# Token slices outermost in the dense units: the loop order of split_unit in a two-layer hybrid decoder step

## What is computed

```python
def ffn(x, norm_g, w_gu, w_down):
    h = rmsnorm(x, norm_g)
    g, u = jnp.split(h @ w_gu, 2, axis=-1)
    return x + (jax.nn.silu(g) * u) @ w_down
...
        x = x + jnp.concatenate([o_nsa, o_ssm], axis=-1) @ w_out    # layer 0
        q, kv = split_cols(h @ w_in, (SWA_WIDTH, SWA_KV_WIDTH))     # layer 1
        x = x + o.reshape(b, L, SWA_WIDTH) @ w_out                  # layer 1
```

## Time and profile before

| | |
|---|---|
| timed runs, median of 3 | 2853.9 us (2848.88 to 2857.44) |
| profiled execution, its own time | 2846.38 us |
| its span, first to last instruction | 2844.7 us |
| mean granted TensorE clock | 0.996 |
| TensorE matmul busy | 2795.5 us (98%) |
| TensorE weight load busy | 2543.5 us (89%) |
| VectorE busy | 1012.2 us (36%) |
| ScalarE busy | 645.6 us (23%) |
| GpSimd busy | 732.7 us (26%) |

### The profile page before, as it was taken

How to read it: one execution, slowest core, us unless ns; L and a number is a source line. 1 busy time by engine, 2 the same in 40 slices (tenths; PEclk the granted TensorE clock), 3 DMA queues, 4 the chain that set the end, 5 groups by cost and what they waited for, 6 DMA issues and landing times.

```text
span 2844.7 us, 44686 instructions
## 1 busy us (share of the span) xinstructions
PE 2795.5 (98%) x18772; PEld 2543.5 (89%) x18772; DVE 1012.2 (36%) x2137; ACT 645.6 (23%) x1344; POOL 732.7 (26%) x495
## 2 busy tenths in 40 slices
PE   8999999999999999999999999999999999999999
PEld 6866676667689999999999999879999999999998
DVE  3122356776553322222222251383432222222224
ACT  4021223666532100000000031284200000000004
POOL 1430000212322222222222231244222222222221
PEclk9999999999999999999999999999999999999999
DMA  7764112100631111111111112100111111111111
GB/s 236 196 178 148 51 31 67 46 29 1 197 108 45 45 45 45 45 45 45 45 45 45 45 45 51 39 17 16 45 45 45 45 45 45 45 45 45 45 60 64
DMA packets 205898, 179.73 MB, mean 63 GB/s; under 512 B 36730, under 2 KB 186287, under 8 KB 205106
## 3 DMA queue, kind: packets, MB, share of 16 engines
q1 hardware_dynamic: 195184, 144.20, 17.0%
q0 software_dynamic: 7616, 30.14, 3.5%
q10 hardware_dynamic: 2898, 2.54, 0.3%
HBM read 162.44 MB, written 19.51 MB: 64 GB/s over the span
## 4 chain that ended last, share of the span: by engine, by line
PE 71%; DVE 2%; ACT 1%; issue 0%; POOL 0%; DVEq 0%; POOLq 0%; ACTq 0%
PE ps L2262 55%; PE ps L2278 4%; PE ps L2298 4%; PE ps L2966 1%; PE ps L2686 1%; PE ps L2546 1%; PE ps L2667 1%; PE ps L2650 1%; PE ps L1911 1%; PE ps L1899 1%; PE ps L1946 0%; DVE arena L2775 0%; DVE arena L2373 0%; PE ps L1928 0%; PE ps L2957 0%
## 5 line engine op out<-in xcount | busy, mean ns | idle before, releaser
L2262 PE MATMUL ps<-spot,w_hi 128*128 128x368 f32 (+1 forms) x6156 | 1185.3, 327 | 1.5 <-DVE arena L2389 0.8
L2262 PEld LDWEIGHTS ps<-spot,w_hi 128*128 128x128 f32 x6156 | 1035.4, 188 | 2.3 <-DVE arena L2389 1.4
L2262 PE MATMUL ps<-spot,w_lo 128*128 128x368 f32 (+1 forms) x3132 | 686.0, 327 | 0.0
L2262 PEld LDWEIGHTS ps<-spot,w_lo 128*128 128x128 f32 x3132 | 537.3, 188 | 0.0
L2231 POOL CAST w_hi<-arena 128x2048 fp32r<-128x2048 f32 x78 | 151.8, 1946 | 1337.0 <-DMA arena<-in_w_gate_up 761.8
L2239 POOL TENSOR_TENSOR w_lo<-arena,w_hi 128x2048 fp32r<-128x2048 f32 x77 | 359.5, 4669 | 6.2
L2389 DVE TENSOR_TENSOR arena<-arena,ps 128x368 f32<-128x368 f32 (+1 forms) x312 | 147.0, 526 | 426.3 <-PE ps L2262 354.9
L601 PE MATMUL ps<-arena 128*128 128x368 f32 (+1 forms) x768 | 241.3, 472 | 0.0
L2487 ACT ACTIVATE arena<-arena 128x1088 f32<-128x1088 f32 x44 | 49.0, 1114 | 831.4 <-DVEq L2503 831.4
L601 PEld LDWEIGHTS ps<-arena 128*128 128x128 f32 x768 | 144.9, 191 | 86.0 <-issue 3.6
L2507 DVE TENSOR_TENSOR arena<-arena,ps 128x368 f32<-128x368 f32 x132 | 62.3, 527 | 443.5 <-PE ps L2262 438.3
(11 more groups left out here) (465 smaller groups left out, 3003.3 us busy)
## 6 DMA issues: line engine op xcount, KB each, us to landing
arena<-in_w_gate_up SPq DMA_DIRECT2D x88, 512.0 KB, 4.7
arena<-in_w_down SPq DMA_DIRECT2D x22, 1024.0 KB, 4.9
arena<-in_cache_nsa_slc_kv SPq DMA_DIRECT2D x112, 128.0 KB, 2.6
arena<-in_cache_nsa_cmp_kv SPq DMA_DIRECT2D x109, 128.0 KB, 2.3
arena<-in_w_in_even SPq DMA_DIRECT2D x9, 1024.0 KB, 7.1
x_spill<-arena POOLq DMA_DIRECT2D x1, 4352.0 KB, 14.2
arena<-in_x_prompt SPq DMA_DIRECT2D x8, 512.0 KB, 6.4
arena<-in_cmp_w_k POOLq DMA_DIRECT2D x16, 256.0 KB, 4.3
```

Of the source, the lines that this page charges most:

```text
L2262: mm = nc.tensor.matmul(ps[:, 3 * s + j, 0:b - a], w, x[:, a:b], start=m == 0, stop=m == len(order) - 1)
```

## The change

In `split_unit` the loop over the three slices becomes the outermost one. For each slice, all of k and hh, hl, lh run, and then the next slice follows. The optional hook `before` would be called in the first slice alone. `start` and `stop` of the accumulation keep their conditions, now once for each slice's own sequence. The other functions are the same.

```diff
@@ -2253,12 +2253,12 @@
 
             E.unit_start(s)
             order = [(kind, k) for k in range(n) for kind in ("hh", "hl", "lh")]
-            for m, (kind, k) in enumerate(order):
-                if before:
-                    before(kind, k)
-                (wh, wl), (xh, xl) = w_of(k), x_of(k)
-                w, x = {"hh": (wh, xh), "hl": (wh, xl), "lh": (wl, xh)}[kind]
-                for j, (a, b) in enumerate(SPLIT):
+            for j, (a, b) in enumerate(SPLIT):
+                for m, (kind, k) in enumerate(order):
+                    if before and j == 0:
+                        before(kind, k)
+                    (wh, wl), (xh, xl) = w_of(k), x_of(k)
+                    w, x = {"hh": (wh, xh), "hl": (wh, xl), "lh": (wl, xh)}[kind]
                     mm = nc.tensor.matmul(ps[:, 3 * s + j, 0:b - a], w, x[:, a:b], start=m == 0, stop=m == len(order) - 1)
             mm.then_inc(unit_ready[s], 1)
 
```

## The result

| | before | changed |
|---|---|---|
| timed runs, median | 2854.7 us (5 runs, 2848.9 to 2871.3) | 2840.8 us (5 runs, 2836.0 to 2842.7) |
| ratio of the runs | | 0.9944, 95% interval 0.9916 to 0.9972 |
| profiled execution, span | 2844.7 us | 2840.9 us |
| same pair timed again later | 2849.9 us (22 runs, 2841.4 to 2866.4) | 2843.6 us (12 runs, 2837.0 to 2848.6) |
| ratio, again | | 0.9986, 95% interval 0.9973 to 0.9998 |

Ratios and intervals are those on record; the quotients of the medians are 0.9951 and 0.9978. The change made the kernel a little faster, by 0.6% in the first comparison and by 0.1% in the second (the two intervals reach from 0.0 to 0.8%), where I had forecast 2859 us, no measurable difference, and a chance of 0.12 for faster. 2840.8 us lies just under the range (2842 to 2873).

What follows compares the result with a forecast made beforehand. TensorE's matmul spacing at L2262 was taken as the bound. Kept counts, waits and weight loads cost 0; the interpolated spacing adds 12.5 us to the profiled 2846.4 us, giving 2859 us, range 2842 to 2873.

Steps and rivals of the forecast that it cites:

- What bounds the kernel: TensorE, busy 98% of the span; an edit to L2262 in `split_unit` can change only the spacing of its matmuls.
- part 1: What is kept in `split_unit`: 9504 matmuls, as many loads, all waits and releases, the other engines' orders; cost nothing.
- the eviction cover: Three eviction additions, 1.43 us, stay hidden behind the next unit, at least 2.96 us; if lost, up to 1.43 us per unit.
- Part 2, weight loads: In `split_unit` the old order saves no loads, one per matmul, so alternating weights lose nothing: cost 0.
- Part 3: In `split_unit`, runs of matmuls into one PSUM bank at one width: no penalty or bonus from the bank; width sets the spacing.
- the sum: All 9504 matmuls at L2262 go from 1567.1 to 1579.6 us, +12.5 us, all on the path.
- a straight line through 320 and 384 columns: Spacing at L2262 interpolated from `final_chunk` rows: 168.6 ns at 368 columns, 161.5 at 352, 166.2 on average.
- rival C: Faster: `split_unit` holds 164.4 ns everywhere, so 1872 slow matmuls gain 4.3 us, giving 2842 us; chance 0.12.
- the 7.5 us between the profiled execution and the median: Possibly one long stretch of some 4000 matmuls at 166.7 instead of 164.4 ns, 9 us; a uniform rhythm would replace this draw.
- A: Slower: every unit of `split_unit` at 166.9 ns, +19.1 us, 2865.5 us in a profile, median near 2871 to 2873; chance 0.22.
- B: Nothing changes: spacing at L2262 ignores bank and neighbours, rhythm still drawn at interruptions; 2846 to 2854 us, chance 0.16.
- D: Loads bind: alternating weights make each L2262 matmul wait for its 188 ns load, +220 us, 3066 us; chance 0.02.

Runs made afterwards that it cites:

- after: The changed kernel itself, slices outermost in `split_unit`, against the kernel before: median 2840.8 us, ratio 0.9944.
- hh_lh_hl: Changed kernel with products in the order hh, lh, hl, so neighbours share data instead of weights: median 2846.6 us, ratio 0.9986 to the kernel before.
- pair01: Against the kernel before, `split_unit` in two passes: both 368-column slices in turn, sharing weights, then the 352-column slice alone; 2867.2 us, ratio 1.0062.
- pair_rot: Like pair01, but slice 1 runs one product ahead of slice 0, so those neighbours share no weights: 2865.4 us, ratio 1.0066 to the kernel before.
- wide: Changed kernel with slices of 384, 384 and 320 columns, lead units and evictions too: median 2863.8 us, ratio 1.0035.
- b_again: The kernel before, unedited, profiled a second time: median 2854.3 us, ratio 1.0005, profiled span 2852.4 us.
- kinds_inner: Against the kernel before, `split_unit` runs the three products next to each other for each block and slice: median 2846.1 us, ratio 0.9976.
- rotated: Kernel before with its slice order kept, but the product turning along with the slice at each matmul: 2849.1 us, ratio 0.9992.
- first_unit: Kernel before with slices outermost only in the one unit that follows each pair of lead units: median 2847.8 us, ratio 0.9992.
- combined: kinds_inner order in `split_unit` and `lead_down`, plus slices outermost in the second unit of `lead_pair`: median 2847.8 us, ratio 0.9989 to the kernel before.

## Why the prediction was wrong

*What bounds the kernel, and part 1:* right. Idle time, counts, waits and the busy time of the other engines stayed; the eviction cover held.

*Part 2, weight loads:* right. The Trainium skill (TensorE: Matmul & The Clock Gate, Part 2) says that one can load the weights once and multiply many times, which spoke against this order; this program does so neither before nor after. There are 6156 and 3132 loads as before, one for each matmul, and orders in which neighbours share or don't share weights gave the same spacing (after and hh_lh_hl; pair01 and pair_rot).

*Part 3 and the sum:* here it failed. The step was "a straight line through 320 and 384 columns", which gave 168.6 ns at 368, 161.5 at 352 and 166.2 on average. The changed kernel shows 166.0 at 368, 160.8 at 352, and 164.3 to 164.5 on average, so it was the value at 368, two slices of three, that was mis-sized by 2.6 ns. The two ends were right (wide measured their 166.2 ns in the very place), and at 360 the line would have been right too; but nothing in the rows showed that 368 lies on it. The term was +12.5 us; measured on the profile it was -3.7 us, almost the price of rival C, "the uniform stream locks into the fast rhythm", -4.3 us. I gave C 0.12 because I set the 384-column rows, which have the larger surcharge, against it.

*Profile against median:* I said that the 7.5 us between the profiled execution and the median could be the draw of a long stretch. Such draws exist: b_again has one, 7.7 us longer in the span. That this was the reason for the 7.5 us isn't shown, since the granted clock and the front move the time by as much. The consequence was drawn only half. If the gap is the draw and the change removes the draw, the changed kernel's median should lie near its own profile and the *whole* gap is gained. Rival C's 2842 us is 0.4% under the median of before, between the 0.6 and 0.1% that were measured. Its number was good, with some luck, since the medians of the changed kernel were 2840.8 and 2843.6 us; its chance was not.

*Rivals A, B and D:* A's spacing of 166.9 ns came true for another order, two slices in turn, and not for this one. B fell: the new order is not a draw, in two profiles of the change and one each of two relatives. D fell.

What makes the rhythms is open. The runs exclude as the sole cause equal widths (pair01 is slow, kinds_inner fast with mixed widths), shared weights (pair_rot), changing operands (rotated) and a state of the chip that lasts through an execution (b_again and first_unit have both rhythms). They leave the sequence of slices, with their widths, starts and banks, and a dependence on what went before, for combined has another value than kinds_inner. The tiles that are read may have a part too, for the output projection of layer 0 has a spacing of its own in most orders. How the two medians' distance divides is open: the first pair of medians differs by 13.9 us, the second by 6.3. A gain of 5 us behind the front is seen against two profiles of the kernel before and 11 us against the third, and 5 to 7 us at equal clock. Mean granted clocks of single runs of the kernel before went from 0.992 to 1.000, and the wait for weights at L597 reached 13.6 us in one profile and isn't listed in another, so part of the first difference is likely chance.

## What to carry to other kernels

If a stream of matmuls is the bound, divide the length of its stretches in the chain by their counts, stage by stage. If the same code has two spacings, each constant to 0.1 ns, a measured time may be a draw, and a single profile is one of them. Take at least two profiles of the baseline before you price a small change. When a gain is below the spread of the runs, compare from the first changed instruction to the end, and compare runs of equal granted clock. Don't interpolate the spacing between widths; run the width.

## What was not expected of the hardware

The spacing of float32r matmuls with a weight load each, at a granted clock of 1.00, took only a few values in the long stretches with slices of 368, 368 and 352 columns, each kept for at least 130 us: 164.1, 164.3 to 164.5, 165.2, 166.7 and 166.9 ns, by order and by draw. In one profile (first_unit) a single unit of 72 matmuls in another order went with the fast rhythm in the 216 matmuls behind it, which were slow in three profiles without it.
